# A fused decoder layer with 32 experts: blocks in loops of three, an earlier weight queue, and down-projections split into halves and quarters of the array

## The reference

```
h = rmsnorm(x) ; proj = h @ w_in                      # 1024 x 1536
ya = gelu(u) * (tril(W_s) @ layernorm(gelu(v)) + b)   # in chunks of 128 positions
yb = (trailing means over 2/4/8/16 tokens - p) @ b_w * scale
x  = x + concat(ya, yb) @ w_out
h2 = rmsnorm(x) ; top group of 4, then top 2 of its 8 experts, gates by softmax
x  = x + sum over the 2 experts of gate * (silu(h2 @ w1[e]) * (h2 @ w3[e])) @ w2[e]
y  = rmsnorm(x)
```

## Time and profile before

| | |
|---|---|
| runs | 980.4, 981.95, 984.45 us |
| the profiled execution, its own time | 978.98 us |
| its span, first to last instruction | 977.4 us |
| granted TensorE clock, mean | 0.969 |
| TensorE matmuls busy | 891.6 us (91%) |
| TensorE weight loads busy | 588.6 us (60%) |
| VectorE, ScalarE, GpSimd busy | 256.4, 110.1, 154.7 us |
| HBM traffic | 272 GB/s over the span |

### The profile page before, as it was taken

How to read it: one execution, slowest core, us unless ns; L and a number is a source line. 1 busy time by engine, 2 the same in 40 slices (tenths; PEclk the granted TensorE clock), 3 DMA queues, 4 the chain that set the end, 5 groups by cost and what they waited for, 6 DMA issues and landing times. The chain is left out here.

```text
span 977.4 us, 24109 instructions
## 1 busy us (share of the span) xinstructions
PE 891.6 (91%) x10538; PEld 588.6 (60%) x10538; DVE 256.4 (26%) x772; ACT 110.1 (11%) x173; POOL 154.7 (16%) x232
## 2 busy tenths in 40 slices
PE   5999999999999995799999999999999989999940
PEld 2545555454554563677778677866767667686720
DVE  1443454625445356150010101101010101001006
ACT  0210111101011011101001000010101000100104
POOL 1000100000000000211313221322223122131110
PEclk9999999999999998699999999999999999999985
DMA  8770200201021027799999999999999999999838
GB/s 333 280 296 1 87 25 18 86 0 43 0 86 44 3 90 287 304 397 376 368 391 389 402 397 398 390 402 392 408 392 402 395 406 390 404 393 400 340 77 324
DMA packets 57484, 259.36 MB, mean 265 GB/s; under 512 B 10809, under 2 KB 11889, under 8 KB 40356
## 3 DMA queue, kind: packets, MB, share of 16 engines
q1 hardware_dynamic: 47484, 238.51, 61.0%
q0 software_dynamic: 9264, 19.36, 8.0%
q10 hardware_dynamic: 640, 0.07, 0.1%
HBM read 240.86 MB, written 25.04 MB: 272 GB/s over the span
## 5 line engine op out<-in xcount | busy, mean ns | idle before, releaser
L1241 PEld LDWEIGHTS ps<-hT,big 128*64 128x64 f32 x8192 | 292.6, 138 | 45.7 <-issue 44.1
L1241 PE MATMUL ps<-hT,big 128*64 128x80 f32 (+2 forms) x8192 | 300.0, 235 | 19.5 <-issue 17.5
L1264 PE MATMUL ps<-big,poolT 128*80 128x512 f32 (+2 forms) x512 | 191.7, 595 | 1.0 <-issue 0.7
L1138 PE MATMUL ps<-big,hT 128*128 128x512 f32 x384 | 169.5, 601 | 3.6 <-DMA big<-in_w_in 2.3
L1138 PEld LDWEIGHTS ps<-big,hT 128*128 128x128 f32 x384 | 73.1, 192 | 94.7 <-issue 88.4
L1264 PEld LDWEIGHTS ps<-big,poolT 128*80 128x80 f32 (+2 forms) x512 | 64.0, 149 | 104.1 <-issue 101.7
L1033 DVE TENSOR_TENSOR poolT<-u,ps 128x320 f32<-128x320 f32 (+2 forms) x32 | 15.5, 486 | 406.1 <-PE ps L1241 406.1
L552 POOL DMA_INDIRECT x_rows<-xn,sidx x32 | 47.2, 1476 | 363.0 <-ACT xn L732 271.4
L529 POOL DMA_INDIRECT slot_table<-ids,dest x18 | 18.9, 1048 | 303.3 <-DVE dest L849 300.3
L1195 PE MATMUL ps<-big 128*128 128x512 f32 x128 | 56.4, 593 | 0.9 <-DVE big L919 0.9
L1211 PE MATMUL ps<-big 128*128 128x512 f32 x128 | 57.0, 598 | 0.0
(11 more groups left out here) (175 smaller groups left out, 499.6 us busy)
## 6 DMA issues: line engine op xcount, KB each, us to landing
big<-in_exp_w SPq DMA_DIRECT2D x192, 1024.0 KB, 24.4
big<-in_w_in SPq DMA_DIRECT2D x4, 1536.0 KB, 13.3
big<-in_w_out SPq DMA_DIRECT2D x2, 2048.0 KB, 14.9
x_rows<-big SPq DMA_DIRECT2D x8, 512.0 KB, 2.6
h_rows<-xn SPq DMA_DIRECT2D x8, 512.0 KB, 2.9
big<-x_rows SPq DMA_DIRECT2D x8, 512.0 KB, 6.8
out_y_prompt<-big SPq DMA_DIRECT2D x8, 512.0 KB, 2.8
big<-in_x_prompt SPq DMA_DIRECT2D x1, 3072.0 KB, 11.8
```

The costliest lines, as they stand in the source:

```text
L1138: last = pe.matmul(ps[0:m, bank, :], hT[:, k, 0:m], win[:, k, part * AW:(part + 1) * AW], start=(k == 0), stop=(k == KD - 1))
L1241: last = pe.matmul(out[c * w:(c + 1) * w, j, 0:m], up_weights(n)[:, k, j * P + c * w:j * P + (c + 1) * w], xT[:, 4 * half + k, 0:m], start ...
L1264: last = pe.matmul(ps[first:first + m, 5 + cols, :], hhT[:, 2 * half + k, 0:m], down_weights(n)[:, k, cols * 512:(cols + 1) * 512], start= ...
```

## The change

1. **Loops.** All engines run the blocks as triples: blocks 0 to 2 unrolled with caps (96, 96, 96), a Fori loop of 6 rounds with caps (96, 80, 64), one of 3 rounds with (80, 80, 64), and a last pair (80, 64). Semaphore counts are computed from the loop's register. The counts of each cap stay 9, 13 and 10. Indices, gates, rows and outputs have three buffers each, so that a buffer belongs to a place in the triple; the third ones are junk and the former band tensors. To sort the experts into this order, VectorE builds a small table turn_row in eight operations in step 7 of the first stage.
2. **Weights.** The wait of SyncE for the first gather is gone. In the loop, SyncE reads the three experts of a triple first and then issues their 18 chunks, each behind its own wait for used.
3. **Down-projections.** In every block rows 0 to 63 are done in array halves; with a cap over 64 the other 16 or 32 rows are done in quarters of the array, each for 256 of the 1024 columns, into PSUM bank 7. The output is scaled by ScalarE and VectorE together in every block, with two more small pieces on each for the other rows.

```diff
-SORTED_CAPS = (96,) * 6 + (80,) * 13 + (64,) * 10
-TURNS = [at for big in range(FIRST // 2) for at in (big, FIRST - 1 - big)] + [FIRST // 2]
-CAPS = [CAP] * SETS + [SORTED_CAPS[at] for at in TURNS]
+CLASSES = ((1, 7, (96, 80, 64)), (7, 10, (80, 80, 64)))
+TURNS = ((1, 7, ((0, 1), (6, 1), (28, -1))), (7, 10, ((12, 2), (13, 2), (22, -1))))
+FINAL, FINAL_CAPS, LEFT = 10, (80, 64), 18
...
+        def triples(eng, block_triple):
+
+            block_triple(0, (CAP,) * SETS)
+            for lo, hi, caps_of in CLASSES:
+                with eng.Fori(lo, hi) as h:
+                    block_triple(h, caps_of)
+            block_triple(FINAL, FINAL_CAPS)
...
-            sp.wait_ge(rows_in[0], 16)
+            def load_weights(h, blocks):
+
+                turn = [sp.value_load(order[0:1, bass.ds(h * SETS + (s - SETS), 1)], min_val=0, max_val=NE - 1)
+                        for s in range(blocks)]
+                for n in range(blocks * CH):
+                    s, c = n // CH, n % CH
+                    before = CH * (SETS * h + s - SETS) + c + 1
+                    sp.wait_ge(used, before if isinstance(h, int) else sp.to_reg(before))
+                    load_chunk(turn[s], n)
+
             sp.wait_ge(out_b, NT)
             for n in range(CH, 10):
                 load_chunk(FIRST + 1, n)
...
-            for b in range(SETS, NE):
-                at = TURNS[b - SETS]
-                turn = sp.value_load(order[0:1, at:at + 1], min_val=0, max_val=NE - 1)
-                for c in range(CH):
-                    sp.wait_ge(used, CH * (b - SETS) + c + 1)
-                    load_chunk(turn, CH * (b % SETS) + c)
+            with sp.Fori(1, FINAL) as h:
+                load_weights(h, SETS)
+            load_weights(FINAL, len(FINAL_CAPS))
...
+                    if m > NS:
+                        for q in range(2):
+                            act.activation(ys[s][NS:m, 256 * q:256 * q + 256],
+                                           ps[QUARTER * q:QUARTER * q + m - NS, 7, 0:256],
+                                           ACT.Copy, scale=gslot[s][NS:m, 0:1])
+                    act.activation(ys[s][0:NS, 0:512], ps[0:NS, 5, :], ACT.Copy,
+                                   scale=gslot[s][0:NS, 0:1]).then_inc(y_ready, 1)
...
+                    for half in range(2):
+                        n = CH * s + 4 + half
+                        pe.wait_ge(chunk_in[n], h * 16 + 16)
+                        for k in range(2):
+                            for cols in range(2):
+                                last = pe.matmul(ps[NS * cols:NS * cols + NS, 5 + cols, :], hhT[:, 2 * half + k, 0:NS],
+                                                 down_weights(n)[:, k, cols * 512:(cols + 1) * 512],
+                                                 start=(half + k == 0), stop=(half + k == 2), skip_group_check=True)
+                            for q in range(4) if m > NS else ():
+                                last = pe.matmul(ps[QUARTER * q:QUARTER * q + m - NS, 7, 0:256], hhT[:, 2 * half + k, NS:m],
+                                                 down_weights(n)[:, k, q * 256:(q + 1) * 256],
+                                                 start=(half + k == 0), stop=(half + k == 2), skip_group_check=True)
                         last.then_inc(used, 1)
```

More of the change, by code:

```diff
@@ L56 @@
 AX = mybir.AxisListType.X
-def in_halves(m):
-    return m <= NS
-HALVES = [sum(in_halves(m) for m in CAPS[:b + 1]) for b in range(NE)]
 def reached(eng, sem, n):
@@ L70, in reached, with not_first @@
         eng.wait_ge(sem, n)
+def not_first(h, s=0):
+    return not (isinstance(h, int) and h == 0) or s > 0
 def build(nc, x_prompt, x_sample, state_pool, norm1_g, w_in, a_norm_g, a_norm_b, ws_sht, bs_th,
@@ L95, in build @@
         chunk = [big[:, c * CHW:(c + 1) * CHW] for c in range(SETS * CH)]
-        own = 2 * CH * CHW
-        xres = big[:, own:own + NT * D].rearrange("p (j d) -> p j d", d=D)
-        yT = big[:, own + NT * D:own + (NT + 1) * D].rearrange("p (k n) -> p k n", n=P)
-        vg, p, ya, ptail = [big[:, own + (NT + 1) * D + i * AW:own + (NT + 1) * D + (i + 1) * AW] for i in range(4)]
-        done_early = sb("done_early", [P, D + 3 * AW])
+        third = 2 * CH * CHW
+        xres = big[:, third:third + NT * D].rearrange("p (j d) -> p j d", d=D)
+        yT = big[:, third + NT * D:third + (NT + 1) * D].rearrange("p (k n) -> p k n", n=P)
+        vg, p, ya, ptail = [big[:, third + (NT + 1) * D + i * AW:third + (NT + 1) * D + (i + 1) * AW] for i in range(4)]
+        done_early = sb("done_early", [P, D + 4 * AW])
         h2T = done_early[:, 0:D].rearrange("p (k n) -> p k n", n=P)
@@ L119, in build @@
         g2t = sb("g2t", [P, KD])
-        ab = sb("ab", [P, AW])
         gf = sb("gf", [P, D])
@@ L476, in _ @@
                         sp.dma_start(chunk_dst(c, c), chunk_src(e, c)).then_inc(ov_w, 16)
-            for s in range(2):
-                sp.wait_ge(rows_out[s], 16 * (NE // 2))
+            for s in range(SETS):
+                sp.wait_ge(rows_out[s], 16 * len(range(s, NE, SETS)))
             sp.wait_ge(state_moved, 16)
@@ L942, in _ @@
             take_hT(0, P)
-            dve.wait_ge(filled, 7)
+            dve.wait_ge(filled, 8)
             pipeline(dve, step)
@@ new lines, in block_triple @@
+            def block_triple(h, caps_of):
+                for s, m in enumerate(caps_of):
+                    b = h * SETS + s
+                    pe.wait_ge(xgT_ready, b + 1)
+                    if not_first(h, s):
+                        pe.wait_ge(hhT_ready, b)
+                    for part, out in enumerate((up1, up3)):
+                        for half in range(2):
+                            n = CH * s + 2 * part + half
+                            pe.wait_ge(chunk_in[n], h * 16 + 16)
+                            for k in range(4):
+                                for j in range(KF):
+                                    for c in range(SPLIT):
+                                        w = P // SPLIT
+                                        last = pe.matmul(out[c * w:(c + 1) * w, j, 0:m],
+                                                         up_weights(n)[:, k, j * P + c * w:j * P + (c + 1) * w],
+                                                         xT[:, 4 * half + k, 0:m], start=(half + k + j == 0),
+                                                         stop=(half + k == 4), skip_group_check=True)
+                            last.then_inc(used, 1)
+                            if not not_first(h, s) and part + half == 0:
+                                pe.wait_ge(onehot_ready, 1)
+                                pe.matmul(ps[0:1, 4, 0:NE], key_own[0:FIRST, 0:1], oh[0][0:FIRST, :], start=True,
+                                          stop=True).then_inc(keys_done, 1)
+                    if not isinstance(b, int) or b + 1 < NE:
+                        pe.wait_ge(rows_in[(s + 1) % SETS], h * 16 + (32 if s == SETS - 1 else 16))
+                        turn(xg[(s + 1) % SETS], P, xgT_done)
+                    if not_first(h, s):
+                        pe.wait_ge(y_ready, b)
+                        pe.wait_ge(y_half_ready, b)
+                    pe.wait_ge(hhT_ready, b + 1)
+                    for half in range(2):
+                        n = CH * s + 4 + half
+                        pe.wait_ge(chunk_in[n], h * 16 + 16)
+                        for k in range(2):
[7 more added lines that the diff above has]
+                                                 start=(half + k == 0), stop=(half + k == 2), skip_group_check=True)
+                        last.then_inc(used, 1)
```

259 lines of the change are left out of this document (123 added, 136 removed).

## The result

The changed kernel takes **1046.01 us** (median of 4 runs, 1042.28 to 1048.04), the kernel before 982.22 beside it (980.4 to 984.45): ratio 1.0654, 95% interval 1.0618 to 1.0690. The forecast was 976.5, the range 966 to 991. The profiled execution has a span of 1046.3 us.

The account below looks back on a forecast made before the run. TensorE and DMA were taken as both full. DMA's later end, less the down-projection work after the last landing, moved TensorE's end from 941.2 to 936.3 (-4.9); with -0.6 for the tail, -5.5: median 976.5 us, range 966 to 991.

Parts of the forecast that it names:

- I take 1.5 us a branch, 10 in all: TensorE's block loops: 7 taken branches at 1.5 us each add 10 us; ends of the range 0.2 and 6.0 us.
- rival 4: TensorE's loops: a taken branch refetches code through a full DMA queue, 6.0 us, 7 times, 42; 998 us; chance 0.10.
- DMA's limit: Expert stage's end: DMA's last landing at 934.5 us, plus 1.8 of down-projection, sets TensorE's end at 936.3.
- TensorE at full share: Sign in the new trace, with no DMA waits, that the forecast is wrong and rival 3 or 4 holds.
- rival 2: Weight queue restarting from empty: DMA 7% below its later rate for 70 us, +5 us, cancelling the gain; 981.5 us; chance 0.20.
- The first block starts 8 us later: Start of expert stage: early weights slow table loads by 4.1 us and first gather by 4.7, less 0.8.
- DMA then ends 3 us later: Weight transfers: pause of 15.5 us instead of 10, with 2.5 us of other traffic moved into it.
- 6.0 us: Down-projection over 64 rows in halves and quarters: 5.2 to 10.5 us, taken as 6.0 with switches, against 7.0 now.
- The expected 22 to 40 us don't come out, because DMA is full: TensorE's saving from down-projections in 22 blocks, 22 us or 40 at the lower end, is hidden by full DMA.
- Loops of the other engines, register loads, evacuation: Other engines' loops, SyncE's three register loads and the small output pieces lie beside TensorE's work; evacuation counted as covered.
- the forecast's signs: New trace if right: PE waits for weights 10 us or more, DMA share 1.0 to about 930, first up-projections near 411.
- Rival 3: TensorE stays the bound, starts later, down-projection stays at 7.0 us: ends at 947 to 957, +8; 990 us; chance 0.17.

Follow-up runs that it names:

- pe_unrolled: The changed kernel with TensorE's loops alone unrolled, the other engines keeping theirs: 982.15 us, ratio 1.0022 to the kernel before.
- pe_unrolled_full: As pe_unrolled, with down-projections of over 64 rows at full width again, evacuated in two column halves: 984.89 us, ratio 1.0046 to the kernel before.
- all_unrolled: The changed kernel with the blocks unrolled on every engine, SyncE too: 982.91 us, ratio 1.0033 to the kernel before.
- before_no_wait: The kernel before with only SyncE's wait for the first gather taken away: 987.57 us, ratio 1.0076.
- loop_full_wait: The changed kernel, loops kept, with down-projections of over 64 rows at full width and SyncE's wait for the first gather restored: 984.02 us, ratio 1.0032.
- loops_misplaced: loop_full_wait with 150 idle TensorE instructions ahead of the first loop and none between the two: 1003.4 us, ratio 1.0232 to the kernel before.
- loops_placed: loop_full_wait with 55 idle TensorE instructions ahead of the first loop and 50 between the two: 974.01 us, ratio 0.9927 to the kernel before.
- light_weights: The changed kernel with only a quarter of each weight chunk transferred from block 3 on, code kept: 993.99 us in one run.

## Why the prediction was wrong

**The step that failed: "I take 1.5 us a branch, 10 in all".** The branch measured 5.8 us (median) and 9.1 with what it brings, 64 in all. The range of the price did hold the branch itself (0.2 to 6.0), and rival 4 described it, with the gap at every third block by which it was to be told, but at 998 us, with a chance of 0.10 and outside the range. Three things were off. First, the short loop of the earlier trace rows was taken as the near case and single stalls of unrolled code as the next; neither has a body that exceeds what stays resident, and code packets all along the stage should have weighed more. Second, rival 4 priced only the branch, 42 us for seven. But the array stood idle for 7.0 us in the case above, in two pieces, and for 53 in seven; and the lower clock behind each stall (2.9 us there, some 14 in seven) was in no term: 64 us came. Third, the forecast let DMA's limit stand, while stalls of 7 to 9 us in every 58 to 62 keep the queue short (landing in 8.3 us, not 27.0): from there on TensorE's every microsecond reaches the end. The cover that hid 22 us of savings can't hide a loss larger than itself. Of the signs for rival 4, no DMA waits and gaps at every third block came; "TensorE at full share" did not, since the gaps themselves empty it. The sign for rival 2, a rate under 380 GB/s, came as well, but with the branches it is gone (398 GB/s in pe_unrolled).

The Trainium skill, "Runtime: NRT & Kernel Launch", section Instruction fetch mechanics, states that code is fetched in blocks of 16 KiB, 256 instructions. The packets here and the border between loops agree with that. It also gives a window of two pages for a taken branch; here bodies that touch 5 to 7 such blocks branch in 0.2 us, so page and measurement differ, and the measurement decides.

**"The first block starts 8 us later"**: right, 7.84, by the terms it was made of: the table loads 4.1 us slower, the gather 3.0 (4.7 less 0.8 in the sum). **"DMA then ends 3 us later"**: wrong, 8.6. The head start was counted as kept; the pause behind it and the thin queue (share 0.88) take it back, and rival 2, which had 5 us for that, was right on this part. Alone, the line costs 7.3 us.

**"6.0 us" for a down-projection over 64 rows**: 6.3, by its terms a half group of 1.01 and a quarter group of 0.57, not 0.87 and 0.44 with a switch; each gives 0.7 us, 16 in all, not 22. **"The expected 22 to 40 us don't come out, because DMA is full"**: right in the main, some 2.7 come out (pe_unrolled_full).

**Loops of the other engines, register loads, evacuation**: nothing, as predicted (all_unrolled). Not foreseen: plan_overflow stands behind the first block's output on VectorE and holds up block 1 by 1.3 to 1.8 us.

**The sum without the branches**: the forecast was set by DMA, so it should hold for pe_unrolled too, at a span of 971.9; it has 979.6. Step by step from the kernel before: +7.3 for the early issue (before_no_wait), -2.7 for what is neither loop, quarter nor issue (new order of blocks, third buffer set, last block of 64 rows: pe_unrolled_full against before_no_wait), -2.7 for the quarters: +1.9, from 980.3 to 982.15. The two steps of 2.7 are about as large as what their intervals leave open. The forecast had -5.5, with +3 for the early issue. Rival 2's 981.5 would have been right for a change without loops. Of the forecast's signs, PE waited for weights for 4.6 us in pe_unrolled, not for 10 or more. (Rival 3's sum has a slip: 947 to 957 against 941.2, less 0.6, is +10 in the middle, not +8.)

## What to carry to other kernels

Ask of a long hardware loop whether its body stays resident on its engine, and look at the duration of the taken branch, not only at the engine's waits, which read "issue". If it doesn't, the price is the fetch, the lower clock behind it, and what falls behind on other queues; unroll, shorten the body, or move it by some dozens of instructions, and put these where the engine waits anyway (0.107 us each here). And a transfer issued earlier gains nothing when it slows the small loads that the next buffer release hangs on: here it cost 7.3 to 8.3 us.

## What the runs showed of the hardware

- A body of 1,697 TensorE instructions branched in 0.2 us or in 7.1 to 7.4 by its place alone: touching 7 packets of 256 instructions it was resident in all six loops that were run so, touching 8 it was fetched again, in loop_full_wait at both taken branches and in loops_misplaced at every other one. Why there only at every other is open. The changed kernel's bodies (8 and 9 packets) were fetched at every one, for 5.8 to 6.4 us.
- Each dear branch brought 9 packets: 97 were fetched with 7 such branches in code of 34 packets, and 50 with two against 32 without.
- With DMA at a share of 0.45 the refetch still took 4.2 us (3.8 to 4.6).
- After two idle stretches of 2.7 and 4.3 us with 15 matmuls between them TensorE's next 241 matmuls took 13.0 us (10.1 at full clock), with a granted clock of 0.50 in the first 3.75 us.
- A wait on a semaphore that is long satisfied, two to an instruction, took 0.107 us an instruction on TensorE (149 recorded in 15.9 us).
- Matmuls of 64 rows on whole 128-column weights take 14.5 us a block, in two halves 7.7; for 16 rows in quarters a group of eight took 0.62 us, for 32 rows 0.64.
- The same 64-row up-projections took 7.69 us in loop_full_wait and 8.7 in loops_placed, whose code lies 55 instructions later (105 in the second loop). A round is 49.0 us long there, not 47.8. With the idle instructions this may be why the resident loops are no better than the unrolled form; no experiment was made on it. The place of the code is not the whole of it: with the changed kernel's code the same group took 7.7 us in light_weights and 8.0 to 8.9 beside full weight traffic.
